# Half of a merge's products moved from behind a recurrence into its pairs, and the gates' sigmoids moved into the walk

## The reference, cut to what matters

```
o_a = nsa_mixer(...)            # 512 tokens x 512
o_b = rwkv7_mixer(...)          # 512 tokens x 512
merged = sigmoid(gate_a) * (o_a @ w_proj_a) + sigmoid(gate_b) * (o_b @ w_proj_b)
x = x + merged @ w_out
```

```
sa    = state @ a_t
state = state * w_t + outer(sa, b_t) + outer(v_t, k_t)
y_t   = state @ r_t
```

## Time and profile before

| what | us |
|---|---|
| median of 3 runs | 1862.84 |
| lowest and highest run | 1862.66, 1864.25 |
| the profiled execution | 1865.49 |
| its span in the trace | 1863.7 |
| PE busy in the span | 1804.5 |
| DVE busy | 783.8 |
| ACT busy | 445.9 |
| POOL busy | 1260.7 |

### The profile page before, as it was taken

The page is one execution under the profiler, slowest core; times in us unless marked ns, Lnnn a source line. Parts: engine busy times, 40 slices in busy tenths (PEclk is TensorE's granted clock), DMA queues, the critical chain, the costliest instruction groups (busy, mean ns, idle before and its releaser), DMA issues.

```text
span 1863.7 us, 29319 instructions
## 1 busy us (share of the span) xinstructions
PE 1804.5 (97%) x11429; PEld 1435.9 (77%) x11429; DVE 783.8 (42%) x1401; ACT 445.9 (24%) x903; POOL 1260.7 (68%) x621
## 2 busy tenths in 40 slices
PE   8999999998899999999999999998889999999998
PEld 7888888876577888888777875666767888888887
DVE  5333360068475333300445344425646355555201
ACT  3000010045431000000322255544524231212000
POOL 8888887854259888877586442232466777877773
PEclk9999999999999999999999999999999999999999
DMA  5222233231023222233342531140024333332331
GB/s 187 101 91 101 94 94 100 80 108 67 23 68 102 101 101 90 94 94 106 127 176 97 164 127 60 45 159 14 4 95 174 94 98 93 98 98 90 94 98 60
DMA packets 60076, 180.32 MB, mean 97 GB/s; under 512 B 7203, under 2 KB 14243, under 8 KB 59084
## 3 DMA queue, kind: packets, MB, share of 16 engines
q1 hardware_dynamic: 49852, 164.71, 26.8%
q10 hardware_dynamic: 10128, 14.25, 2.2%
HBM read 165.81 MB, written 13.13 MB: 96 GB/s over the span
## 4 chain that ended last, share of the span: by engine, by line
PE 92%; DVE 3%; ACT 2%; issue 2%; DMA 0%; ACTq 0%; DVEq 0%
PE bank L567 25%; PE bank L569 25%; PE bank L568 25%; PE bank L993 1%; PE bank L1021 1%; PE bank L966 1%; PE bank L1182 1%; PE bank L585 1%; PE bank L589 1%; PE bank L586 1%; PE bank L928 1%; PE bank L1154 1%; PE bank L1167 0%; DMA x_tok<-x_dram 0%; DVE sc L2094 0%
## 5 line engine op out<-in xcount | busy, mean ns | idle before, releaser
L475 POOL TENSOR_TENSOR w_hi<-w_raw,one 128x1024 fp32r<-128x1024 f32 (+1 forms) x279 | 527.2, 1890 | 466.1 <-PE bank L569 406.0
L477 POOL TENSOR_TENSOR w_lo<-w_raw,w_hi 128x1024 fp32r<-128x1024 f32 (+1 forms) x279 | 682.7, 2447 | 21.9
L567 PE MATMUL bank<-h_hi,w_hi 128*128 128x512 f32 x1392 | 551.2, 396 | 4.7 <-DVE xT L1981 1.6
L568 PE MATMUL bank<-h_lo,w_hi 128*128 128x512 f32 x1392 | 542.7, 390 | 0.0
L569 PE MATMUL bank<-h_hi,w_lo 128*128 128x512 f32 x1392 | 542.7, 390 | 0.0
L567 PEld LDWEIGHTS bank<-h_hi,w_hi 128*128 128x128 f32 x1392 | 261.7, 188 | 66.5 <-issue 7.7
L568 PEld LDWEIGHTS bank<-h_lo,w_hi 128*128 128x128 f32 x1392 | 261.6, 188 | 57.1 <-issue 3.8
L569 PEld LDWEIGHTS bank<-h_hi,w_lo 128*128 128x128 f32 x1392 | 261.7, 188 | 55.0
L567 PE MATMUL bank<-a_hi,w_hi 128*128 128x512 f32 x528 | 205.5, 389 | 0.0
L569 PE MATMUL bank<-a_hi,w_lo 128*128 128x512 f32 x528 | 205.4, 389 | 0.0
L568 PE MATMUL bank<-a_lo,w_hi 128*128 128x512 f32 x528 | 205.4, 389 | 0.0
(11 more groups left out here) (394 smaller groups left out, 2175.4 us busy)
## 6 DMA issues: line engine op xcount, KB each, us to landing
w_raw<-w_ffn_gu_dram SPq DMA_DIRECT2D x88, 512.0 KB, 3.3
w_raw<-w_conv_up_dram SPq DMA_DIRECT2D x44, 512.0 KB, 3.5
w_raw<-w_ffn_down_dram SPq DMA_DIRECT2D x32, 448.0 KB, 3.2
w_raw<-w_ffn_down_dram SPq DMA_DIRECT2D x16, 512.0 KB, 3.5
w_raw<-w_out_dram SPq DMA_DIRECT2D x16, 512.0 KB, 3.4
w_raw<-w_gates_dram SPq DMA_DIRECT2D x16, 512.0 KB, 3.6
w_raw<-w_rwkv_dram SPq DMA_DIRECT2D x14, 512.0 KB, 3.4
w_raw<-w_conv_down_dram SPq DMA_DIRECT2D x16, 448.0 KB, 3.2
```

Of the source, the lines that this page charges most:

```text
L475: nc.gpsimd.tensor_tensor(w_hi[:, s, 0:width], raw, one[:, 0:1].to_broadcast([P, width]), ALU.mult).then_inc(sem("w_rounded"), 1)
L477: nc.gpsimd.tensor_tensor(w_lo[:, s, 0:width], raw, w_hi[:, s, 0:width].bitcast(F32), ALU.subtract).then_inc(sem("w_split"), 1)
L567: nc.tensor.matmul(dst, hi, rhs_hi[:, k, :], start=start and k == k0, stop=False)
L568: nc.tensor.matmul(dst, hi, rhs_lo[:, k, :], start=False, stop=False)
```

## The change

Six of the merge's eight tiles get their first half (attention's heads) multiplied inside pairs 1 to 3, two tiles in a pair, 24 products. A generator `heads_products(m)` yields after each product, and `heads_product(n)` takes the next n. In levels 2 to 5 one is taken ahead of each `level_x`; in every level one ahead of half 0's `level_d` (in level 5, where there is none, ahead of `level_dt`); in levels 1 to 4 one ahead of half 1's `level_d`; then one ahead of each ug half; and up to six behind ug, ahead of the wait for its copies, until the 24 are used up. The even tile sums in bank 7, the odd one in bank 6; ScalarE copies each out (`head_aside`) to a place called `aside`, the even one in level 5 and the odd one behind the copies of ug. POOL multiplies the six copies by their sigmoids during the walk.

For this the merge's weights are packed anew: chunks 0 to 3 hold the first halves of two tiles each, chunks 4 to 7 the second halves. POOL splits chunk 0 ahead of pair 0, the heads (`split_heads`) at the end of pair 0's masks, chunks 1 to 3 at the end of the masks of pairs 1 to 3, chunks 4 to 6 behind them, and chunk 7 behind the six multiplications. SP loads the heads ahead of pair 0, a quarter of the gates after pair 2, and the other three quarters after pair 3. ScalarE makes all four sigmoids in the walk, between two table loads. `bonus_sum` moves from level 3 to level 2 and, for pairs 1 to 3, from bank 7 to 6; `bonus_out` from level 4 to level 3. In the merge remain the first halves of tiles 6 and 7, ahead of the wait for the group norm, and the eight second halves. A tile is then gate times second half plus the prepared first half.

```diff
+            def heads_products(m):
+                for t in (2 * m - 2, 2 * m - 1):
+                    c, dst = FIRST["merge"] + m - 1, bank[7 - t % 2][:, :]
+                    if t % 2 == 0:
+                        pe.wait_ge(*nth("w_split", c + 1))
+                        pe.wait_ge(*nth("rw_tok", 4 * m + 4))
+                    elif m < 3:
+                        pe.wait_ge(*nth("bonus_done", m + 2))
+                    else:
+                        pe.wait_ge(*nth("rw_tok", 4 * m + 3))
+                    for k in range(4):
+                        if t == 0:
+                            pe.wait_ge(*nth("o_ready", k + 1))
+                        at = slice((4 * (t % 2) + k) * P, (4 * (t % 2) + k + 1) * P)
+                        hi, lo = w_hi[:, c % RING, at], w_lo[:, c % RING, at]
+                        nc.tensor.matmul(dst, hi, oa_hi[k], start=k == 0, stop=False)
+                        yield
+                        nc.tensor.matmul(dst, hi, oa_lo[:, k, :], start=False, stop=False)
+                        yield
+                        last = nc.tensor.matmul(dst, lo, oa_hi[k], start=False, stop=k == 3)
...
                 for k in range(1, 6):
+                    if k > 1:
+                        heads_product()
                     level_x(m, k, 0)
...
+                    if k > 1:
+                        heads_product()
                     level_x(m, k, 1)
-                    if k == 3 and m < 3:
-                        pe.wait_ge(*nth("rw_tok", 4 * m + 4))
+                    if k == 2 and m < 3:
                         bonus_sum(m + 1)
                     if k == 1:
                         keyed_values(m)
+                    heads_product()
                     if k < 5:
                         level_d(m, k, 0)
                     level_dt(m, k, 0)
                     if k < 5:
+                        heads_product()
                         level_d(m, k, 1)
                 level_dt(m, 5, 1)
                 for half in range(2):
+                    heads_product()
                     pe.wait_ge(*nth(f"dt_ready{half}", 6 * m + 6))
...
+                heads_product(6)
                 pe.wait_ge(*nth("ug_read", 2 * m + 2))
...
+            def head_aside(t):
+                if t % 2:
+                    act.wait_ge(*nth("w_used", FIRST["merge"] + t // 2 + 1))
+                else:
+                    act.wait_ge(*nth("merge_a_done", t // 2 + 1))
+                nc.scalar.activation(aside[t], bank[7 - t % 2][:, :], ACT.Copy).then_inc(sem("merge_a_read"), 1)
...
+                    if k == 5 and m:
+                        head_aside(2 * m - 2)
...
+                if m:
+                    head_aside(2 * m - 1)
                 act.wait_ge(*nth("chunk_terms", m + 1))
...
+            nc.scalar.preload_act_table(ACT.Sigmoid)
+            merge_gate("gates_in", gates_b0[:, :, :])
+            merge_gate("gate_in_a0", gates_a[:, 0:4, :])
+            merge_gate("gate_in_a1", gates_a[:, 4:8, :])
+            merge_gate("gate_in_b1", gates_b1[:, :, :])
             logs()
...
-            nc.scalar.preload_act_table(ACT.Sigmoid)
             head_hi(2)
-            merge_gate(0)
             head_hi(3)
-            for j in range(1, 4):
-                merge_gate(j)
...
+            for u in range(3):
+                split_merge(RING + u)
+            for t in range(ASIDE):
+                pool.wait_ge(*nth("merge_gate", 2 + t // 4))
+                pool.wait_ge(*nth("merge_a_read", t + 1))
+                nc.gpsimd.tensor_tensor(aside[t], aside[t], gates_a[:, t, :], ALU.mult)\
+                    .then_inc(sem("merge_a_scaled"), 1)
+            split_merge(RING + 3)
```

More of the change, by code:

```diff
@@ L441, in _ @@
             sp.wait_ge(*nth("chunk_terms_copied", 4))
[L442 to L446, removed]
+            load_gates(gates_a[:, 0:4, :], 0, "gate_in_a0")
+            load_gates(gates_a[:, 4:8, :], 1, "gate_in_a1")
+            load_gates(gates_b1[:, :, :], 3, "gate_in_b1")
             sp.wait_ge(*nth("x_out", 16))
@@ L1059, in bonus_sum @@
                 pe.wait_ge(*nth("rk_product", m + 1))
-                nc.tensor.matmul(bank[7][:, :], head_ones2, sq[:, 1, :], start=True, stop=True)\
+                if m:
+                    pe.wait_ge(*nth("kk_sum", m + 1))
+                nc.tensor.matmul(bank[6 if m else 7][:, :], head_ones2, sq[:, 1, :], start=True, stop=True)\
                     .then_inc(sem("rw_head_sum"), 1)
@@ L1184, in level_dt, with heads_product @@
                 last.then_inc(sem("level_dt"), 1)
+            def heads_products(m):
[8 more added lines that the diff above has]
+                        pe.wait_ge(*nth("rw_tok", 4 * m + 3))
+                    for k in range(4):
+                        if t == 0:
[7 more added lines that the diff above has]
+                        last = nc.tensor.matmul(dst, lo, oa_hi[k], start=False, stop=k == 3)
+                        if k == 3:
+                            last.then_inc(sem("w_used" if t % 2 else "merge_a_done"), 1)
+                        yield
+            beside = [iter(())]
+            def heads_product(n=1):
+                for _ in range(n):
+                    next(beside[0], None)
             for m in range(4):
                 AtV, Bt, Kt, Vt = pair_sets[m % 2][3:]
+                if m:
+                    beside[0] = heads_products(m)
                 if m == 0:
@@ L2382, in bonus_out @@
                 dve.wait_ge(*nth("rw_head_sum", 2 * m + 2))
-                nc.vector.tensor_tensor(bonus[:, m, :], bank[7][:, :], pin[:, 8 + m, :], ALU.mult)\
+                nc.vector.tensor_tensor(bonus[:, m, :], bank[6 if m else 7][:, :], pin[:, 8 + m, :], ALU.mult)\
                     .then_inc(sem("bonus_done"), 1)
@@ L2725, in _layouts @@
     part = lambda a, b: blocks(w2[:, a:b])
-    merge = np.concatenate([blocks(one["w_proj_a_2"]), blocks(one["w_proj_b_2"])], 2)
+    merge = np.concatenate([np.concatenate([w[0::2], w[1::2]], 2)
+                            for w in (blocks(one["w_proj_a_2"]), blocks(one["w_proj_b_2"]))])
     pe = [one[n].reshape(16, P).T for n in ("cmp_pe_k_2", "cmp_pe_v_2")]
```

144 lines of the change are left out of this document (97 added, 47 removed).

## The result

| | median of runs | profiled execution, span |
|---|---|---|
| before | 1862.75 us (4 runs, 1860.58 to 1864.25) | 1863.7 |
| changed | 1873.99 us (4 runs, 1871.45 to 1876.95) | 1875.2 |

The ratio is 1.0061, 95% interval 1.0049 to 1.0073. The forecast was 1860.9, its range ended at 1868.5: the change costs 11 us where 1.9 were to be gained. The profiled execution of the changed kernel is the longest of its four, and 5.5 above the shortest. The mean granted clock of the four executions is 0.993 in the profiled one, 0.996 in the shortest and 0.994 in the other two. Over spans of some 1873 us that is, as an estimate, 26, 15, 22 and 22 us at half clock; 11 us more at half clock cost about 6 us, which is the spread.

A forecast was written before the change was run, and what follows sets the result against it. TensorE, holding 92% of the span, was taken as the bound: -16.5 - 1.3 + 27.9 - 6.6 - 4.0 - 1.4 = -1.9 us, 1863.6 profiled, carried to a 1860.9 us median; range 1854 to 1868.5.

The forecast's parts named there:

- The merge's 72 products: Merge: six tiles' first halves leave a TensorE stretch without gaps, 0.229 us per product, -16.5 us.
- the head behind the sigmoid: Before the merge: the last rounded head's copy no longer waits on ScalarE behind a gate sigmoid, -1.3 us.
- VectorE kept up: Merge: VectorE needs 2.3 us per tile, one multiply given to POOL, under TensorE's 2.75; cost 0.
- The issue stops in the levels: Levels of pairs 1 to 3: TensorE's stops for issue vanish, as lone products give the instruction queue time, -4.0 us.
- those in the chunk products: Chunk products of the pairs: the burst of five ahead covers half of 2.9 us of issue stops, -1.4 us.
- the price of a lone product: Pairs 1 to 3: 0.42 us for each product alone between 64x64 groups; all 72 products add +27.9 us.
- absorbed: Pairs 1 to 3: added products fill 6.6 us of idle time and 5.4 of issue stops, 12.0 us together.
- The rule that I had set against the change: Levels: a full-array product among 64-row tiles can't have weights loaded ahead, so its price stays near 0.42, not 0.229.
- "costed at nothing" on SP: SP's queue: heads, gates and chunks load a stage or more earlier, its next jobs wait for splits anyway; cost 0.
- ScalarE in the walk: Walk: two table loads and four sigmoids fit ScalarE's idle time, done at 1400.4 just before the squares; cost 0.
- a rival of 3 us late: Walk: last gates land at 13.6, squares start 3 us late, 1.8 on the path; 1862.7 us, chance 0.10.
- The rival of the other side: Pairs: waits aren't filled, the absorbed 12.0 us return; 1866.9 us with half, 1872.9 with all; chance 0.22.

The follow-up runs named there:

- Experiments 5 and 9: Against the late load, 18 of 19 lone products per pair: each issued twice, 1880.44 us; cut from 512 to 128 columns, F32R on full array, 1858.20 us.
- experiments 6 and 8: Against the late load, 18 lone products per pair on one 64x64 tile: F32R with 512 columns, 1864.24 us; F32 with 128 columns, 1851.82 us.
- experiment 1: Changed kernel with the late load: heads' load, and with it the next merge chunk, issued only after the last write-outs landed; 1864.95 us.
- experiment 4: Changed kernel with the fourth gate sigmoid put back behind the last rounded head, a table load ahead of the last two heads; 1871.55 us.
- experiments 10 to 12: Changed kernel with late load and last sigmoid moved; products in one run 1856.06 us, in runs at the waits 1853.58, in two runs 1854.36.
- experiment 2: Changed kernel with all 24 products of a pair in one run behind the UG groups, ScalarE's two copies after its UG copies; 1865.99 us.

## Why the forecast was wrong

**The right parts.** The merge's 72 products and the head behind the sigmoid: -17.8 forecast, -17.6 measured between the same events. VectorE kept up. The issue stops in the levels went (4.0 forecast); those in the chunk products went too, 2.9 where I took 1.4, though 1.1 of new ones stand in the changed kernel's pair 3. That the stops are waits for instructions is my reading and not shown: the four of pairs 1 and 2 end 1.3 to 1.5 us after a packet of the instruction queue has landed, but such a packet comes every 3 to 6 us in any case. The page "Runtime: NRT & Kernel Launch" of the Trainium skill, section "Instruction fetch mechanics", has fetching as mostly hidden. If the stops are that, it was not hidden in 4.3 us of before's pairs 1 and 2, and was in the changed kernel's (0.0).

**The first failing step: the price of a lone product.** I took 0.42, from the attention stage, with 0.10 to get in and 0.09 to get out, and gave 0.49 as the upper bound. By the starts it is 0.53: entry 0.10 was right, exit is 0.20. That is 60 x 0.11 = 6.6 us; since more was absorbed than forecast (15.6 in place of 12.0 us in three pairs), 2.9 of it are left in the sum. The rest of that account holds: per pair 19 x 0.53 and the run's 1.4 give 11.5, the pair grew by 6.8, so 4.7 went into idle time and stops, against 4.0 forecast. The error was in the choice of row: what follows the run of products in the attention stage is a 128x64 group, not the levels' 64x64 groups, and the bonus sum, which stood inside a level, gave me 0.13 beside its streaming, which I took for one side's price and doubled; the runs show two unlike sides. Experiments 5 and 9 show the 0.30 as something that adds to the streaming. The rule that I had set against the change ("TensorE: Matmul & The Clock Gate" of the Trainium skill, section "Part 3: Packing small matmuls - row/col tiling": loads run beside matmuls only where row groups differ) was right in direction: the price did not fall to 0.229. Row groups alone don't decide it: the products of experiments 6 and 8 use the same one tile, and the next group starts 0.38 behind the one and together with the other.

**The second failing step: "costed at nothing" on SP.** I looked at what was queued behind the moved loads on SP's own queue, and not at what another queue had under way at the moment of their issue. ScalarE's last write-out gates pair 0. That is 5.4 us against before and 6.5 against the late load (experiment 1), the largest part of the 8.8 by which the sum below misses, and in no rival of the forecast. Part of it is the clock: TensorE stood still for 5.9 us up to 1274.9, and the records show it at 1.2 GHz for 10.2 us from 1271.1.

**The third, small: ScalarE in the walk.** I had the last gates landing 10.7 after 1386.5, which is 11.9 after the walk's start, and the squares just in time, with a rival of 3 us late and 1.8 of it on the path. The last gates landed 12.4 after the walk's start (9.7 after their issue), and the squares began 15.7 after it where before they began 15.4 after it. In the traces that costs 0.3 in walk and group norm together. With the walk at full clock on both sides it would be the group norm's 1.5, of which moving one sigmoid gives back 1.2 (experiment 4): within the bound, and not the nothing that I chose.

**The rival of the other side** (waits aren't filled) gave nearly the right time (1872.9) for a wrong reason, which is luck: the waits were filled in the changed kernel. But in experiments 10 to 12 filling them brought no gain over a run behind UG that could be told from noise, so its core, that a product in a level postpones what hangs behind it, has more for it than a chance of 0.22. No run shows that core by itself.

In sum: with the changed kernel's pair 3 at full clock (experiment 1) the pairs cost 6.85 + 6.57 + 5.4 = 18.8 (forecast 15.9), pair 0 5.4 (0), walk and group norm 0.3 (0), the merge -17.6 (-17.8): +6.9 where the forecast had -1.9. The fall of the clock in pair 3 adds 6.4 in the profiled execution. By the forecast's own way of carrying over, +6.9 gives 1869.7; the median is 4.3 above it. The three other executions have no trace, but their mean clocks do: two had some 22 us at half clock, as the estimate above has it, where the profiled one without its pair 3 has 13.7. Those 8 us cost about 4. Where in these executions the clock fell stays open.

## What to carry to other kernels

A full-array product put alone between groups of 64x64 float32 matmuls cost its streaming and 0.30 us here, so put such products in runs and count the changes, not the products. A run put into a wait brought nothing here that could be told, so ask what hangs behind the place that it fills. Before a load is moved ahead, look at every queue's transfers at its new place, and ask what waits for them: 1.5 MB ahead of 256 KB cost 6.5 us on the path.

## What the hardware did that I had not expected

- Getting out of a lone product takes 0.19 to 0.20 us, getting in 0.10, whether it has 128 or 512 columns. Another shape alone suffices (0.11 in, 0.20 out); with another type in one tile it was 0.10 in and 0.15 out, at 512 columns. With type and shape the same, at 128 columns, the product starts together with the next group.
- A 256 KB write-out took 8.1 us behind 1.5 MB that had been issued within 0.6 us ahead of it on another queue, and 2.0 without. Its first packet started 4.1 us after its issue in the one case and 0.8 in the other.
- Stops for issue in dense runs of small matmuls, 4.3 us in pairs 1 and 2, were gone with lone products among them (0.0). With one run of 24 per pair they were 0.6 in experiment 2, but 3.9 in its pair 3, where before had 2.6.
- In the four kernels with the early load TensorE idled for 4.4 to 5.9 us in pair 0. The granted clock fell to half 2.1 to 3.4 us into that and stood there for 10.2 us, the last 6.4 to 8.2 of them with TensorE at work again; without that wait it stood at half in pair 0 for at most 3.4.
- A stretch of 3.4 us at half clock cost 1.3 us in the walk (13.4 against 12.1), and two such stretches 3.1 to 3.6 together ahead of pair 0 (its start in the traces with two and with none).
